# Longer contiguous runs for the expert weights of a fused two-block transformer kernel on one core

## The reference, cut to what matters

```python
h2 = modulate(rms_norm(x, g_norm2[l]), sh2, sc2)      # * (1 + sc2) + sh2
x = x + ga2[:, None, :] * hierarchical_moe(h2, w_rg[l], b_rg[l], w_re[l], b_re[l], w1[l], w3[l], w2[l])
...
g_logits = (xt @ w_rg).astype(jnp.float32) + b_rg      # 4 groups, top 1
e_logits = ((xt @ w_re).astype(jnp.float32) + b_re)    # 32 experts, top 2 of the 8 of the group
...
hid = jax.nn.silu(xb @ w1[e]) * (xb @ w3[e])           # w1, w3: (32, 1024, 512)
return hid @ w2[e]                                     # w2: (32, 512, 1024)
```

## Time and profile before

| | |
|---|---|
| time, median of 3 runs | 1341.48 us (1341.46 to 1341.81) |
| profiled execution, own time | 1341.16 us |
| its span, first to last instruction | 1339.2 us |
| PE busy | 1196.7 us, 89% |
| DVE, ACT, POOL busy | 535.3, 390.1, 275.5 us |
| mean granted TensorE clock | 0.943 of full speed |
| read from memory | 329.83 MB, 247 GB/s over the span |

### The profile page before, as it was taken

The page is one execution under the profiler, slowest core; times in us unless marked ns, Lnnn a source line. Parts: engine busy times, 40 slices in busy tenths (PEclk is TensorE's granted clock), DMA queues, the critical chain, the costliest instruction groups (busy, mean ns, idle before and its releaser), DMA issues.

```text
span 1339.2 us, 15394 instructions
## 1 busy us (share of the span) xinstructions
PE 1196.7 (89%) x5840; PEld 790.5 (59%) x5840; DVE 535.3 (40%) x987; ACT 390.1 (29%) x576; POOL 275.5 (21%) x115
## 2 busy tenths in 40 slices
PE   4879879897999999998999998877999989999988
PEld 2668657675444433333343436866777768888866
DVE  1595643533112111111111115799755624333224
ACT  2533234311111111111111115442344435444332
POOL 1341122400000000000000003353611524442531
PEclk7798879998999999999999999888988989999998
DMA  9845537574999999999999995331331445554540
GB/s 321 296 147 189 183 131 277 212 280 157 394 394 394 394 394 394 394 394 395 395 395 395 394 395 199 126 126 64 126 126 64 138 134 176 189 188 160 187 156 32
DMA packets 154450, 331.55 MB, mean 248 GB/s; under 512 B 3609, under 2 KB 26418, under 8 KB 154402
## 3 DMA queue, kind: packets, MB, share of 16 engines
q1 hardware_dynamic: 153328, 330.23, 67.1%
q0 software_dynamic: 288, 0.47, 0.3%
q10 hardware_dynamic: 786, 0.19, 0.1%
HBM read 329.83 MB, written 1.05 MB: 247 GB/s over the span
## 4 chain that ended last, share of the span: by engine, by line
PE 54%; DMA 22%; DVE 14%; SPq 6%; issue 3%; ACT 2%; DVEq 0%; ACTq 0%
DMA ring<-in_w 18%; PE ps L736 11%; PE ps L737 11%; PE ps L738 11%; PE ps L1018 11%; SPq L633 4%; DMA ring<-in_w_ada 3%; PE ps L1045 2%; PE ps L1005 2%; DVE ring_r L1708 1%; SPq L644 1%; DVE acc L1774 1%; DMA ring<-in_w_in 1%; PE ps L1114 1%; PE ps L787 1%
## 5 line engine op out<-in xcount | busy, mean ns | idle before, releaser
L700 POOL TENSOR_TENSOR ring_r<-ring,ring_r 128x1024 fp32r<-128x1024 f32 x88 | 231.4, 2650 | 1000.6 <-ACT ring_r L1308 1000.6
L1018 PE MATMUL ps<-ring,arena 128*64 128x512 f32 x1024 | 225.9, 595 | 19.2 <-DMA ring<-in_w 17.4
L737 PE MATMUL ps<-ring_r,hl_r 128*128 128x512 f32 x528 | 216.1, 409 | 0.0
L736 PE MATMUL ps<-ring_r,hl_r 128*128 128x512 f32 x480 | 201.3, 419 | 4.4 <-DVE hr_r L1792 2.2
L738 PE MATMUL ps<-ring_r,hr_r 128*128 128x512 f32 x480 | 194.9, 406 | 0.0
L1308 ACT ACTIVATE ring_r<-ring 128x2048 fp32r<-128x2048 f32 x90 | 167.1, 1905 | 88.7 <-PE ps L738 55.3
L1018 PEld LDWEIGHTS ps<-ring,arena 128*64 128x64 f32 x1024 | 76.5, 137 | 166.1 <-issue 166.1
L1708 DVE TENSOR_TENSOR ring_r<-ring,ring_r 128x2048 fp32r<-128x2048 f32 x46 | 113.2, 2460 | 116.5 <-ACT ring_r L1308 116.2
L737 PEld LDWEIGHTS ps<-ring_r,hl_r 128*128 128x128 f32 x528 | 104.6, 198 | 22.5
L1976 DVE TENSOR_TENSOR arena<-arena,ps 128x512 f32<-128x512 f32 x16 | 11.0, 688 | 259.2 <-PE ps L1018 259.2
L1045 PE MATMUL ps<-ring,arena 128*64 128x512 f32 x512 | 113.4, 595 | 0.0
(11 more groups left out here) (333 smaller groups left out, 1509.9 us busy)
## 6 DMA issues: line engine op xcount, KB each, us to landing
ring<-in_w SPq DMA_DIRECT2D x96, 2048.0 KB, 19.0
ring<-in_w_in SPq DMA_DIRECT2D x21, 2048.0 KB, 9.1
ring<-in_w_ada SPq DMA_DIRECT2D x12, 2048.0 KB, 11.8
ring<-in_w_ffn_gate SPq DMA_DIRECT2D x11, 1024.0 KB, 5.3
ring<-in_w_ffn_up SPq DMA_DIRECT2D x11, 1024.0 KB, 7.8
ring<-in_w_ffn_down SPq DMA_DIRECT2D x5, 2048.0 KB, 7.8
ring<-in_w_o SPq DMA_DIRECT2D x2, 2048.0 KB, 7.7
ring<-in_w_out SPq DMA_DIRECT2D x2, 2048.0 KB, 8.0
```

The costliest lines, as they stand in the source:

```text
L700: nc.gpsimd.tensor_tensor(rest[:, a:b], w[:, a:b], lead[:, a:b].bitcast(F32), ALU.subtract).then_inc(sem("w_rest_b"), 1)
L736: mm(o, lhsT=a_lead, rhs=b_lead, start=start, stop=False, skip_group_check=True)
L737: mm(o, lhsT=a_lead, rhs=b_rest, start=False, stop=False, skip_group_check=True)
L1018: last = mm(H[slots_of(e), :], lhsT=xs[:, k, slots_of(e)], rhs=wide(MOE_SLOT[2 * n + e])[:, k, :], start=k == 0, stop=k == KD - 1)
```

## The change

The contraction of each expert matmul is summed in another order. A contraction index of 512 rows is now seen as `(p, j)`, index `4p + j`, with `p` the partition and `j` the chunk, so partition `p` holds four consecutive rows. For `w1` and `w3` (1024 rows) this is done for each half `h`, and a partition gets two runs of four rows of 512 floats, 8 KB each; for `w2` one run of four rows of 1024 floats, 16 KB. The bytes and their place in the ring slot (chunk after chunk in the free dimension) stay the same in number and shape, and so do the operands that PE streams.

Everything that meets these chunks must be permuted to match: the columns of `x` in `gather()` and in the transposes for the router, and the columns of `hid` in its transposes. A new function `fourth(row, h, j)` gives every fourth column of a half, 128 columns 16 bytes apart, as the stationary operand. `mod` for the second norm, `g_norm2` and the bias come in the same order: the matmul of line 814 takes strided columns for these, and three new small loads fill `ffnmod`, in place of the rows that `prow` held. `wr` is loaded in four DMAs and not in two.

```diff
+        def fourth(row, h, j):
+            return row[:, h * COL:(h + 1) * COL].rearrange("p (q j) -> p j q", j=4)[:, j, :]
...
         def expert_load(sp_, n, pair, signal):
-            src = expert_w[n][bass.ds(2 * pair + n % 2, 1)].rearrange("e (k p) n -> p (e k) n", p=P)
-            view = tall(MOE_SLOT[n]) if n >= 4 else wide(MOE_SLOT[n])
+            w = expert_w[n][bass.ds(2 * pair + n % 2, 1)]
+            view = ring[:, MOE_SLOT[n], :]
+            if n >= 4:
+                src = w.rearrange("e (p f) n -> p (e f n)", p=P)
+            else:
+                src = w.rearrange("e (h p j) n -> p (e h) (j n)", p=P, j=4)
+                view = view.rearrange("p (h r) -> p h r", h=2)
             sp_.dma_start(view, src).then_inc(signal[MOE_SLOT[n]], 16)
...
-            pool.dma_start(wr[:, :, 0:GROUPS], A["w_rg"][0].rearrange("(k p) n -> p k n", p=P)).then_inc(sem("route_in"), 16)
-            pool.dma_start(wr[:, :, GROUPS:], A["w_re"][0].rearrange("(k p) n -> p k n", p=P)).then_inc(sem("route_in"), 16)
+            for h in range(2):
+                rows = slice(h * COL, (h + 1) * COL)
+                for name, at, n in (("w_rg", 0, GROUPS), ("w_re", GROUPS, EXPERTS)):
+                    pool.dma_start(wr[:, 4 * h:4 * h + 4, at:at + n],
+                                   A[name][0, rows].rearrange("(p j) n -> p j n", p=P)).then_inc(sem("route_in"), 16)
+            for n, src in enumerate((A["b_ada"][0, 3 * D:4 * D], A["b_ada"][0, 4 * D:5 * D], A["g_norm2"][0, :])):
+                pool.dma_start(ffnmod[:, n, :].rearrange("p (h j) -> p h j", h=2),
+                               src.rearrange("(h p j) -> p h j", p=P, j=4)).then_inc(sem("ffnmod_in"), 16)
...
                     for j in range(COL // P):
-                        last = mm(o[:, j:j + 1], lhsT=ada_acc(c)[:, j * P:(j + 1) * P], rhs=ones[:, 0:1], start=True,
-                                  stop=True)
+                        columns = ada_acc(c)[:, j * P:(j + 1) * P] if c < 6 else fourth(ada_acc(c), 0, j)
+                        last = mm(o[:, j:j + 1], lhsT=columns, rhs=ones[:, 0:1], start=True, stop=True)
...
+            def route_transposes(units):
+                for t, h in units:
+                    pe.wait_ge(*x1_ready(t, h))
+                    o = small.claim(pe, f"x1t{t}{h}")
+                    for j in range(4):
+                        last = nc.tensor.transpose(o[:, j * P:(j + 1) * P], fourth(x[:, t, :], h, j), ident)
+                    last.then_inc(small.done, 1)
...
                 for n, G in enumerate((GA, GB)):
                     for j in range(4):
-                        k = 4 * n + j
                         for t in range(TT):
-                            last = mm(G[:, j * P:(j + 1) * P], lhsT=x[:, t, k * P:(k + 1) * P], rhs=S[:, t, :],
+                            last = mm(G[:, j * P:(j + 1) * P], lhsT=fourth(x[:, t, :], n, j), rhs=S[:, t, :],
                                       start=t == 0, stop=t == TT - 1)
...
                 for f in range(FT):
-                    last = nc.tensor.transpose(GA[:, f * P:(f + 1) * P], hid[:, f * P:(f + 1) * P], ident)
+                    last = nc.tensor.transpose(GA[:, f * P:(f + 1) * P], fourth(hid, 0, f), ident)
```

More of the change, by code:

```diff
@@ L57 @@
 C_ALL = C_IOTA + CAP
-PARAM_ROWS = [("c", KD), ("b_ada", 6 * KD), ("g_norm1", KD), ("g_norm2", KD), ("conv_w", 3 * CT), ("conv_b", CT),
+PARAM_ROWS = [("c", KD), ("b_ada", 6 * KD), ("g_norm1", KD), ("conv_w", 3 * CT), ("conv_b", CT),
               ("norm_mix_g_2", KD), ("hg_lb_logits_2", 2 * HG), ("hg_onorm_g_2", 1), ("norm_ffn_g_2", KD),
@@ L182, in two_blocks @@
         scale2 = sb("scale2", [P, KD])
+        ffnmod = sb("ffnmod", [P, 3, KD])
         oghalf = sb("oghalf", [P, 1])
@@ L960, in _ @@
             out_rows("", 0, 1)
-            norm_transposes("x1t", x1_ready, TH[0:2])
+            route_transposes(TH[0:2])
             o = small.claim(pe, "rb")
-            pe.wait_ge(sem("route_in"), 64)
+            pe.wait_ge(sem("route_in"), 96)
             pe.wait_ge(sem("scale2_ready"), 1)
@@ L978, in logits @@
                 last.then_inc(small.done, 1)
-            norm_transposes("x1t", x1_ready, TH[2:3])
+            route_transposes(TH[2:3])
             logits(0)
-            norm_transposes("x1t", x1_ready, TH[3:4])
+            route_transposes(TH[3:4])
             logits(1)
@@ L1845, in _ @@
             dve.wait_ge(sem("mod_raw"), 8)
-            link(v.tensor_tensor(mod[:, 3 * KD:5 * KD], mod[:, 3 * KD:5 * KD], pc("b_ada", 3 * KD, 2 * KD), ALU.add))
-            v.scalar_tensor_tensor(scale2[:, :], mod[:, 4 * KD:5 * KD], 1.0, pc("g_norm2"), ALU.add,
+            dve.wait_ge(sem("ffnmod_in"), 48)
+            link(v.tensor_tensor(mod[:, 3 * KD:5 * KD], mod[:, 3 * KD:5 * KD], ffnmod[:, 0:2, :].rearrange("p a k -> p (a k)"),
+                                 ALU.add))
+            v.scalar_tensor_tensor(scale2[:, :], mod[:, 4 * KD:5 * KD], 1.0, ffnmod[:, 2, :], ALU.add,
                                    ALU.mult).then_inc(sem("scale2_ready"), 1)
             dve.wait_ge(sem("scale2_ready"), 1)
-            dve.wait_ge(sem("route_in"), 64)
+            dve.wait_ge(sem("route_in"), 96)
             small.ready(dve, "pv7")
```

## The result

The changed kernel takes 1386.39 us (median of 4 runs, 1383.8 to 1387.55), against 1341.47 us before: a ratio of 1.0336 (95% interval 1.0317 to 1.0355), 3.4% slower. The forecast was 1320 us, 1.6% faster, with a range up to 1342. The rival told as "strided weight loads at half pace", to which I had given 0.14, said 1387.

What follows compares the result with a forecast made beforehand. Expert-stage transfers (31.92 us a pair), close above PE (30.20), were taken as the bound. 1341.16 - 19.9 - 2.5 + 0 + 0.5 = 1319.3 us, with 0.3 for the median 1319.6, told as 1320; range 1316 to 1342.

Steps and rivals of the forecast that it cites:

- strided weight loads at half pace: Rival: each weight load of the gather takes its 114 ns twice, a pair 34.2 us; about 1387 us; chance 0.14.
- part 1: Expert stage: faster loads end PE's waits for `w3`, leaving PE's pace; -19.9 us, between -19.9 and -17.6, or 0.
- Length of run: Expert loads: 8 KB runs reach 423 GB/s, 16 KB 429, so a pair's transfers take 29.6 us, under PE's 30.20.
- part 2: End of the expert stage: `fq` lands before ACT is free, so its splits end earlier; -2.5 us, bounds -3.3 and 0.
- part 3: Gather and transposes: stationary columns 16 bytes apart cost 0; upper bound +3.6 and +0.4 us per pair.
- part 4: Head: POOL's five more DMAs load the DMA engines before the first modulation chunk; +0.5 us, between -0.5 and +2.

Runs made afterwards that it cites:

- the sweep: Kernel before, with the gather's column groups at steps of 1 to 8 floats and `w2` matmuls streaming at steps 1, 2, 4, 8: 1425.47 us (one run).

## Why the prediction was wrong

*The waits for `w3`* (part 1, -19.9 us): right as a mechanism and in size, but PE's new length hid it in the changed kernel. With the gather contiguous the waits are gone and the period is 30.20 us. In the kernel with only the gather contiguous, the second half of the last `up` begins at 771.00 + 13.88 / 2 = 777.9, and its first pair 1.7 us later than before (317.92 against 316.18); less that, it is the forecast's 776.2.

*Length of run*: right. 29.66 us against 29.6 forecast. One thing the rows did not show: SP's issue of an expert load lasted 2.67 us in the median before, up to 7.50, and lasts 0.38 with the change; in the chain of before 3.91 us of it stand ahead of the transfer at us 424.78. It did not set the pace: with the stride alone, the same loads in the same runs are issued in 0.43 us in the median, where PE sets the pace.

*The end of the stage* (part 2, -2.5 us): right, and it is in the changed kernel as well. From the start of the last `w2` matmuls to PE's first split matmul of the next block it was 15.5 us and is now 12.8 us (856.77 to 869.60 in the chain above). The chain of before there:

```profile
808.88 7.04 PE ps L1045 x32
...
824.42 0.23 PE ps L736
```
ACT, POOL and DVE with the change, answering to the earlier trace rows (start us, us):

```profile
855.87 3.70 ACT L1331 ACTIVATE ring_r<-ring 128x2048 fp32r<-128x2048 f32 x2
```

```profile
859.64 4.67 POOL L716 TENSOR_TENSOR ring_r<-ring,ring_r 128x1024 fp32r<-128x1024 f32 x2 [594.44 <-ACT ring_r L1331]
```

```profile
864.60 2.29 DVE L1731 TENSOR_TENSOR ring_r<-ring,ring_r 128x2048 fp32r<-128x2048 f32 x1
866.81 0.22 DVE L2019 TENSOR_TENSOR wfs_r<-wfox,wfs_r 128x64 fp32r<-128x64 f32 x1
```

ACT starts on `fq` right after its last copy, POOL ends at 864.3, and the small subtraction takes 0.22 us where it took 2.36.

*The stationary operands* (part 3, taken as 0): this step failed. The upper bound stood there, +3.6 us for the gather per pair, and the measured cost is +3.90, still above the bound. I had taken 0 with the reason that a float32 weight load of 192 ns, against 140 of a transpose, shows that the fetch has room. The runs show the opposite: both kinds suffer, 192 to 330 ns and 140 to 208, and the gather took 3.6 us of loads in 3.8 us of matmuls, so nothing covers a slower one. Without a row of a strided stationary operand, the value nearest to 0 was a guess, and the point that I worked out for it (1.3 us a gather) was small beside the bound. The sign of the whole hung on that, and deserved more than 0.14.

*The rival's own sum*: it put the last second half of `up` at us 839.8. It began at 833.32 + 13.88 / 2 = 840.3. The mechanism is the rival's, but that the sum came so near is in part luck. It had 34.2 us a pair for the measured 34.09 (3.6 for the gather's 3.9, and 0.4 for the transposes of `hid`, which cost nothing: PE waits there for DVE's 1.38 us (L1990) anyway), and 3.6 us before the first pair, where head and gather together came to 2.7. These errors of 2.5 us in all were made up by 3.0 us in the first pair, which it did not foresee: `up` took 16.91 us there and 13.95 before.

*The head* (part 4, +0.5): the modulation load that the chain first waits for starts 0.9 us later (19.15 against 18.29), inside the bounds of -0.5 to 2, and the last experiments show by moving POOL's queue that this is its part. The first gather starts 1.2 us later (309.40 against 308.24), but in the profiled executions of the kernels with the same queue it starts anywhere from 307.4 to 310.9, so that figure tells little.

The sum of the profile: head and first gather 2.7 us (318.87 against 316.18), from the start of the first pair to that of the last 43.1 (514.45 against 471.4, where the last pair of before starts at 787.55), in the last pair 2.1 (its gather 3.9 longer, less the 1.8 that its wait for `w3` had cost), the end -2.7: 45.2 us up to the next block. Of the 43.1, 3.0 fall in the first pair: the granted clock was 0.50 (1.2 GHz) from us 318.8 to about 324.5, after 1.75 us in which PE waited for DVE, and 1.00 (2.4 GHz) in the same place before, after the same wait. The kernel with the stride alone and the sweep lost 1.7 us each there, those that gather contiguous columns or every second one nothing; whether the stride brings it is open. The last 1.2 us to 46.4 came in the second block: 516.0 us from its first split matmul to the end, against 514.8. Four executions with the same second block and a contiguous gather took 511.3 to 514.6, so 1.2 us is within what executions differ by.

## What to carry to other kernels

Before a layout is permuted to suit the DMA, follow each operand that must be permuted to match to the engine that reads it, and price that read: columns of float32 one 16-byte line apart doubled the time of the gather (3.78 to 7.68 us), which is bound by weight loads, and that of the streams in the sweep, while steps of 2 floats were nearly free. If a stage has two limits 6% apart, as 30.2 and 31.9 us here, no more than this gap can be gained by moving the longer one, and what a cost on the other adds beyond the gap is paid in full. A copy in the permuted order, made once on an engine that waits (4.4 us of ACT), kept the gain; and small loads with runs of 16 to 128 bytes belong where no big load is waited for.

## What was not expected of the hardware

A strided gather took no longer at the lower clock. The first gather of the changed kernel ran at a mean granted clock of 0.66 (0.50, that is 1.2 GHz, up to us 313) and took 7.74 us, where later ones at 1.00 take 7.68; the contiguous one took 6.2 us at 0.60 and 3.78 at 1.00. So the first gather lost 1.5 us by the stride and not 3.9.

Moving POOL's small loads, 0.2 MB, away from the first 6 us let the modulation load that the chain first waits for start 2.75 us earlier in the kernel before (15.54 against 18.29), about their share of the DMA engines there (20.5% of 13 us). With the five more of the change it was 4.3 us (15.09 against 19.36 with the copy alone), though their share is no larger (20.1%); why is not shown.

A step of 3 floats costs about half of what a step of 4 adds (259 against 327 and 190 ns).
